# Linear attention: the order of the score-value and state matmuls in a chunk

## The chip, the cores and the metric

The kernel runs on one core of a Trainium2 chip. The metric is the device time of one execution in microseconds (us); lower is better. Engines are named as the profile names them: PE (TensorE), PEld (its weight loads), DVE (VectorE), ACT (ScalarE), POOL (GpSimd), SP (the engine whose queue starts most transfers).

## What is computed

One decoder layer on 512 tokens of width 1024: a mixer with two branches (gated linear attention, GLA, and a sparse softmax attention) and then a mixture of 32 experts. The change touches the GLA branch only. Its reference, cut to one chunk and one head:

```python
b = cumsum(la)                                   # log decay inside the chunk
o_inter = (q * exp(b)) @ state                   # the state carried into the chunk
scores = einsum('td,sd,tsd->ts', q, k, decay)    # causal, decayed
o = o_inter + scores @ v
state = exp(b_last) * state + (k * exp(b_last - b)).T @ v
```

There are 4 heads with 64 key and 128 value columns. The kernel uses chunks of 128 tokens, so there are TT = 4 chunks, numbered 0 to 3.

## The kernel before

All data is fp32. A matmul on plain fp32 operands is executed as two passes, so the profile counts two PE instructions for each of them; weight products are instead written out by hand as three matmuls on rounded operands (lines 480 to 482), one pass each.

The semaphores and the order of work are written by hand, one instruction list for each engine. Softmax attention and GLA are interleaved in one loop over units u = 0 to 16 (line 668). In unit u PE does, in this order: the attention scores of unit u (`attn_scores`, line 588, 64 contraction rows for each of two heads), the transposes of unit u-1 (`attn_turn`, line 598), `gla_out(ch)` if u is 9, 11, 13 or 15 (chunk 0, 1, 2 or 3), one eighth or so of a weight product as filling (lines 480 to 482), `gla_turn(ch-1)` in even units from 10 (line 660), the attention output of unit u-1 (`attn_out`, line 611), and `gla_scores(ch)` in units 8, 10, 12 and 14 (lines 620 and 627). DVE, ACT and POOL walk the same units in their own lists.

`gla_out(ch)` (line 632) is where the change is. It takes the PSUM banks G and O, head pair member hh = 0 writing to G and hh = 1 to O, each in two column halves r = 0 and 1. For each of the four heads it issues, from chunk 1 on, a state matmul (line 642: 64 contraction rows, SBUF rows 0 to 63 for hh = 0 and rows 64 to 127 for hh = 1) and right behind it a score-value matmul (line 643: 128 contraction rows) that adds to the same columns. Then, except in the last chunk, it forms the chunk's contribution to the state (line 652) in one of the banks T0 and T1, which take turns. The profile writes an instruction's rows and columns of the array before the shape: 64\*128, 128\*128 or 128\*64.

What reads the results: ACT squares the four heads of o (line 1441, `gla_squares`), DVE makes the norm (lines 1727, 1951, 1957, `gla_norm`) and frees G and O, DVE updates the state (line 1942), and POOL starts the exponents of the next chunk (lines 1193 and 1195, `gla_exponents`) when both banks are full, because these exponents overwrite the factors that the state matmuls read; line 1206 on POOL follows. ACT copies the first head's transposed probabilities out of a T bank (line 1469, freed at line 1471), DVE the second's (line 1992). ACT copies the attention output out of bank O (line 1481), and `gla_scores` takes G and O after that. DVE scales the probabilities at line 2002.

Weights come through a ring: the SP queue starts the load of an item when PE has signalled that an earlier item is used up (`ring_out`, waited for before line 994 and the lines after it), and the first expert weights (line 1032) wait for the end of the output projection in the same way.

Of the kernel before, what the change touches and what calls it, by code (L numbers as in the profile page):

```python
# [24 lines left out]
P = 128  # L25
# [56 lines left out]
def layer(nc, x, c, positions, w_ada, b_ada, g_pre_mix, g_post_mix, g_pre_ffn, g_post_ffn, w_in,  # L82
# [17 lines left out]
    with ExitStack() as ctx:  # L100
# [20 lines left out]
        expo = qi_mem[:, 0:1792].rearrange("p (r n) -> p r n", r=2)  # L121
# [11 lines left out]
        gv = gvs[:, 0:2048].rearrange("p (t n) -> p t n", t=TT)  # L133
# [23 lines left out]
        scT = gla_mem[:, 1024:1536].rearrange("p (h n) -> p h n", h=4)  # L157
        kN = gla_mem[:, 1536:1792]
        state = gla_mem[:, 1792:2048].rearrange("p (r n) -> p r n", r=2)
# [141 lines left out]
        ps, bank = {}, {}  # L301
# [87 lines left out]
        def _(pe):  # L389
            def take(name, turn):  # L390

                n = bank[name].turn(turn)
                if n:
                    pe.wait_ge(bank[name].free, n)
                return ps[name]
# [3 lines left out]
            def take_next(kind, turn):  # L399
                name = f"{kind}{flip[kind] % 2}"  # L400
                flip[kind] += 1
                where[turn] = name
                return take(name, turn), bank[name].full
# [11 lines left out]
            for k in range(KD):  # L415
                t, full = take_next("T", ("x", k))
                for tt in range(TT):
                    if k == 0:
                        pe.wait_ge(xn_ready, tt + 1)
                    last = nc.tensor.transpose(t[:, tt * P:(tt + 1) * P], x_in[:, tt, k * P:(k + 1) * P], ident[:, :])  # L420
# [108 lines left out]
            for tt in range(TT):  # L529
                a, full = take_next("A", ("small", tt))  # L530
                for k in range(KD):
                    last = nc.tensor.matmul(a[:, 0:NS], hT[:, k, tt * P:(tt + 1) * P], w_small[:, k, :], start=(k == 0), stop=(k == KD - 1))
# [11 lines left out]
            for tt in range(TT):  # L544
                last = nc.tensor.transpose(t[:, tt * P:(tt + 1) * P], kin[:, tt, :, :].rearrange("p a n -> p (a n)"), ident[:, :])
            last.then_inc(full, 1)
            t, full = take_next("T", "ga")
            for tt in range(TT):
                last = nc.tensor.transpose(t[0:RANK, tt * P:(tt + 1) * P], ikw[:, tt, 0:RANK], ident[:, :])
# [14 lines left out]
            for n in range(3 * PAIRS):  # L564
                index_scores(1 + n // PAIRS, n % PAIRS)
                if n in (1, 3):

                    r = n // 2
# [63 lines left out]
            def gla_out(ch):  # L632
                pe.wait_ge(sc_ready, 2 * ch + 2)
                pe.wait_ge(gv_ready, TT)
                o = [take(n, ("o", ch)) for n in ("G", "O")]
                if ch:
                    pe.wait_ge(state_ready, 2 * ch)
                for r in range(2):
                    for hh in range(2):
                        h, lo = 2 * r + hh, 64 * hh  # L640
                        if ch:
                            nc.tensor.matmul(o[hh][:, r * P:(r + 1) * P], expo[lo:lo + 64, r, 640:768], state[lo:lo + 64, r, :], start=True, stop=False)
                        last = nc.tensor.matmul(o[hh][:, r * P:(r + 1) * P], scT[:, h, :], gv[:, ch, h * P:(h + 1) * P], start=(ch == 0), stop=True)
                        if r == 1:
                            last.then_inc(bank["GO"[hh]].full, 1)
                if ch < TT - 1:
                    pe.wait_ge(kN_ready, ch + 1)
                    t, full = take_next("T", ("state", ch))
                    for r in range(2):
                        for hh in range(2):  # L650
                            h = 2 * r + hh
                            last = nc.tensor.matmul(t[64 * hh:64 * hh + 64, r * P:(r + 1) * P], kN[:, r * P + 64 * hh:r * P + 64 * hh + 64],
                                                    gv[:, ch, h * P:(h + 1) * P], start=True, stop=True)
                    last.then_inc(full, 1)
# [13 lines left out]
            for u in range(NU + 1):  # L668
                ch, odd = (u - GLA_AT) // 2, (u - GLA_AT) % 2
                if u < NU:  # L670
                    attn_scores(u)
                if u:
                    attn_turn(u - 1)
                if odd and 0 <= ch < TT:
                    gla_out(ch)
                if fill:
                    fill.pop(0)()
                if not odd and 0 < ch <= TT:
                    gla_turn(ch - 1)
                if u:  # L680
                    attn_out(u - 1)
                if not odd and 0 <= ch < TT:
                    gla_scores(ch)
# [1730 lines left out]
```

## Time and profile before

| what | value |
|---|---|
| three timed runs | 791.08, 793.13, 793.21 us; median 793.13 us |
| the profiled execution: its span | 789.2 us, 9728 instructions |
| PE | 703.0 us busy (89%) |
| PE weight loads | 447.0 us (57%) |
| DVE / ACT / POOL | 411.7 (52%) / 287.7 (36%) / 120.9 us (15%) |
| the GLA chunks' `gla_out` on PE | between 248.3 and 327.6 us of the span |

No other time of the profiled execution is given than its span, which covers the first to the last instruction. The median lies 3.9 us above it. The profile's PE clock is the clock that was granted to TensorE, as a share of 2.4 GHz. A busy PE is not a PE at its peak: a matmul's record lasts from its start to its modelled end and records overlap, so what a matmul costs is read from the distance between starts.

### The profile page before, as it was taken

To read this page: it belongs to the slowest core of one execution; us is meant where nothing else is said; L and a number is where in the kernel's file an instruction comes from. 1 tells how busy PE (TensorE), PEld (TensorE's weight loads), DVE (VectorE), ACT (ScalarE), POOL (GpSimd) and SP (SyncE) were. 2 spreads that over 40 slices of the span, in tenths; PEclk is the share of its full clock that TensorE was granted. 3 is DMA by queue.
4 is the path that set the end of the run, shared out by engine and by line. 5 is a ranking of instruction groups with operands and counts; after the bars stand their busy time and mean duration, and the time that the engine had idled before them with its cause. 6 is when DMAs were issued, how large, how long until landed. Compare 5 with 4: busy or idle time off the path is not lost.

```text
span 789.2 us, 9728 instructions
## 1 busy us (share of the span) xinstructions
PE 703.0 (89%) x3451; PEld 447.0 (57%) x3451; DVE 411.7 (52%) x876; ACT 287.7 (36%) x514; POOL 120.9 (15%) x148
## 2 busy tenths in 40 slices
PE   1799989998998999999999899989979978878784
PEld 0347747666776777777787678873423323323221
DVE  2386858998897665654422636572533211112118
ACT  5233255254447768642022315344112211112223
POOL 3064852210002022000000000101121221111100
PEclk9999989999999889999999999999989998989997
DMA  9989730411302030023334472599999999999982
GB/s 337 396 311 364 283 142 1 116 44 64 107 9 99 1 107 1 5 104 107 107 123 161 142 267 79 229 374 391 418 422 418 420 419 419 421 420 413 409 327 108
DMA packets 50300, 179.27 MB, mean 227 GB/s; under 512 B 9624, under 2 KB 13826, under 8 KB 36428
## 3 DMA queue, kind: packets, MB, share of 16 engines
q1 hardware_dynamic: 44308, 166.26, 54.1%
q0 software_dynamic: 4784, 8.19, 2.9%
q10 hardware_dynamic: 1160, 4.20, 1.4%
q8 instruction: 28, 0.46, 0.2%
q14 instruction: 20, 0.16, 0.1%
HBM read 174.13 MB, written 12.59 MB: 237 GB/s over the span
## 4 chain that ended last, share of the span: by engine, by line
PE 48%; SPq 13%; DVE 13%; DMA 8%; ACT 4%; issue 3%; POOL 0%; DVEq 0%; ACTq 0%; POOLq 0%; PEldq 0%
PE psA L480 10%; PE psA L482 10%; PE psA L481 10%; SPq L1032 5%; SPq L1090 4%; SPq L1040 4%; PE psS L884 3%; PE psA L913 3%; DMA arena<-in_w_e_up_dram 2%; PE psG L884 2%; DVE mk_mem L1846 2%; DMA y_dram<-sig_mem,tables 2%; DVE m L1845 2%; PE psO L611 1%; PE psT L598 1%
## 5 line engine op out<-in xcount | busy, mean ns | idle before, releaser
L480 PE MATMUL psA<-arena_r 128*128 128x512 f32 x320 | 130.8, 409 | 3.5 <-DVE arena_r L1794 2.9
L481 PE MATMUL psA<-arena_r 128*128 128x512 f32 x320 | 127.0, 397 | 0.0
L482 PE MATMUL psA<-arena_r 128*128 128x512 f32 x320 | 126.8, 396 | 0.0
L1794 DVE TENSOR_TENSOR arena_r<-arena,arena_r 128x1024 fp32r<-128x1024 f32 (+1 forms) x37 | 60.4, 1654 | 38.4 <-ACT arena_r L1313 37.4
L480 PEld LDWEIGHTS psA<-arena_r 128*128 128x128 f32 x320 | 61.5, 192 | 24.4 <-issue 12.3
L482 PEld LDWEIGHTS psA<-arena_r 128*128 128x128 f32 x320 | 61.5, 192 | 13.5
L481 PEld LDWEIGHTS psA<-arena_r 128*128 128x128 f32 x320 | 61.5, 192 | 12.2 <-issue 0.2
L884 PE MATMUL psG<-arena,kv 128*64 128x512 f32 x208 | 61.2, 642 | 7.6 <-issue 7.6
L884 PE MATMUL psS<-arena,kv 128*64 128x512 f32 x224 | 58.5, 611 | 9.8 <-issue 7.9
L1313 ACT CAST arena_r<-arena 128x1024 fp32r<-128x1024 f32 (+1 forms) x31 | 49.9, 1630 | 20.6 <-DMA arena<-in_w_in_dram 10.2
L913 PE MATMUL psA<-qs_mem,sig_mem 128*64 128x512 f32 x80 | 39.5, 637 | 4.4 <-ACT sig_mem L1637 4.4
L2291 DVE TENSOR_TENSOR sig_mem<-sig_mem,psS 128x256 f32<-128x256 f32 x8 | 4.9, 613 | 72.7 <-ACT sig_mem L1632 72.7
L1239 POOL DMA_INDIRECT y_dram<-sig_mem,tables x16 | 15.9, 994 | 174.6 <-issue 108.5
L480 PE MATMUL psA<-arena_r,qs_mem_r 128*128 128x512 f32 x96 | 38.1, 397 | 4.2 <-DVEq L2037 3.3
L2291 DVE TENSOR_TENSOR sig_mem<-sig_mem,psG 128x256 f32<-128x256 f32 x8 | 4.9, 612 | 70.7 <-ACT sig_mem L1632 70.7
L884 PEld LDWEIGHTS psS<-arena,kv 128*64 128x64 f32 x224 | 20.1, 140 | 37.4 <-issue 36.9
L884 PEld LDWEIGHTS psG<-arena,kv 128*64 128x64 f32 x208 | 19.6, 147 | 33.5 <-issue 32.8
L472 PE MATMUL psA<-arena,kv 128*128 128x512 f32 x64 | 29.2, 619 | 2.3 <-DMA arena<-in_w_in_dram 2.3
L481 PE MATMUL psA<-arena_r,qs_mem_r 128*128 128x512 f32 x80 | 31.1, 389 | 0.0
L1646 ACT COPY sig_mem<-psA 128x512 f32<-128x512 f32 x16 | 9.4, 586 | 55.7 <-PE psA L913 32.2
L1411 ACT ACTIVATE sig_mem<-psA 128x512 f32<-128x512 f32 x16 | 9.6, 598 | 50.8 <-PE psA L482 50.8
L1845 DVE MAX8 m<-mk_mem 128x8 f32<-128x256 f32 (+2 forms) x48 | 26.9, 560 | 2.2
(443 smaller groups left out, 1304.2 us busy)
## 6 DMA issues: line engine op xcount, KB each, us to landing
arena<-in_w_e_gate_dram SPq DMA_DIRECT2D x24, 1024.0 KB, 17.0
arena<-in_w_e_up_dram SPq DMA_DIRECT2D x24, 1024.0 KB, 19.4
arena<-in_w_in_dram SPq DMA_DIRECT2D x11, 2048.0 KB, 8.8
arena<-in_w_e_down_dram SPq DMA_DIRECT2D x12, 1024.0 KB, 18.6
qs_mem<-in_w_e_down_dram SPq DMA_DIRECT2D x10, 1024.0 KB, 23.0
arena<-in_w_ada_dram SPq DMA_DIRECT2D x4, 2048.0 KB, 16.8
qT<-in_w_ada_dram SPq DMA_DIRECT2D x6, 1024.0 KB, 5.4
gvs<-in_w_ada_dram SPq DMA_DIRECT2D x5, 1024.0 KB, 6.3
```

Of the source, the lines that this page charges most:

```text
L472: last = nc.tensor.matmul(a[:, :], hT[:, k, tt * P:(tt + 1) * P], w[:, k, :], start=(k == 0), stop=(k == KD - 1))
L480: nc.tensor.matmul(acc, lhs[0], rhs[0], start=start, stop=False)
L481: nc.tensor.matmul(acc, lhs[0], rhs[1], start=False, stop=False)
L482: return nc.tensor.matmul(acc, lhs[1], rhs[0], start=False, stop=stop)
L884: last = nc.tensor.matmul(ps[g][64 * q:64 * q + 64, :].rearrange("p (g f) -> p g f", g=2), h2g[:, b, k, 64 * q:64 * q + 64], gu, start=(k ...
L913: last = nc.tensor.matmul(ps[name][64 * q:64 * q + 64, :], actT[:, b, kf, 64 * q:64 * q + 64], down_sets[z][q][:, D * kf + 512 * n:D * kf ...
L1032: sp.dma_start(dst, src[bass.ds(e, 1), :, :].rearrange("a p n -> p (a n)")).then_inc(we_in[z], 16)
L1040: sp.dma_start(down_sets[z][q], wed_v[bass.ds(e, 1), :, :].rearrange("a p n -> p (a n)")).then_inc(wd_in[z], 16)
L1090: sp.dma_start(gu_sets[z][q][:, 2048 * n:2048 * (n + 1)][:, part], src[2 * j + q][:, part]).then_inc(we_last[j - (NPAIR - 2)] if half else ...
L1313: nc.scalar.copy(hi[:, part], src[:, part]).then_inc(hi_ready, 4 if q is None else 1)
L1794: V.tensor_tensor(lo[:, part], src[:, part], hi[:, part], ALU.subtract).then_inc(lo_ready, 4 if q is None else 1)
L1845: step(V.max(m8[:, :], work))
```

## The change

The four score-value matmuls of a chunk come first, the four state matmuls behind them, after the wait for the state (line 637), which moves between the two groups. Each bank is now one accumulation group: the first matmul into a bank has the start flag, all later ones in it, also those on the other column half, have not. The signal that a bank is full moves to the last state matmul of that bank; in chunk 0, which has no state matmuls, it stays on the last score-value matmul. Number, shapes and operands of the matmuls are the same.

```diff
                 o = [take(n, ("o", ch)) for n in ("G", "O")]
+                for r in range(2):
+                    for hh in range(2):
+                        h = 2 * r + hh
+                        last = nc.tensor.matmul(o[hh][:, r * P:(r + 1) * P], scT[:, h, :], gv[:, ch, h * P:(h + 1) * P], start=(r == 0), stop=(ch == 0 and r == 1))
+                        if r == 1 and ch == 0:
+                            last.then_inc(bank["GO"[hh]].full, 1)
                 if ch:
                     pe.wait_ge(state_ready, 2 * ch)
-                for r in range(2):
-                    for hh in range(2):
-                        h, lo = 2 * r + hh, 64 * hh
-                        if ch:
-                            nc.tensor.matmul(o[hh][:, r * P:(r + 1) * P], expo[lo:lo + 64, r, 640:768], state[lo:lo + 64, r, :], start=True, stop=False)
-                        last = nc.tensor.matmul(o[hh][:, r * P:(r + 1) * P], scT[:, h, :], gv[:, ch, h * P:(h + 1) * P], start=(ch == 0), stop=True)
-                        if r == 1:
-                            last.then_inc(bank["GO"[hh]].full, 1)
+                    for r in range(2):
+                        for hh in range(2):
+                            lo = 64 * hh
+                            last = nc.tensor.matmul(o[hh][:, r * P:(r + 1) * P], expo[lo:lo + 64, r, 640:768], state[lo:lo + 64, r, :], start=False, stop=(r == 1))
+                            if r == 1:
+                                last.then_inc(bank["GO"[hh]].full, 1)
```

## Rows read from the trace of the kernel before

**Rows 1.** The page, part 4: the chain that ended last, shares by engine.
```profile
PE 48%; SPq 13%; DVE 13%; DMA 8%; ACT 4%; issue 3%; POOL 0%; DVEq 0%; ACTq 0%; POOLq 0%; PEldq 0%
```
**Rows 2.** Windows: stretch, its length, busy us (instructions) by engine, PEclk, DMA share, GB/s.
```profile
160.00:345.00 185.00, 175.88 (x1013) 132.13 (x1009) 140.67 (x346) 108.85 (x219) 18.70 (x21) 0.95 0.16 58
537.00:760.00 223.00, 192.04 (x908) 73.66 (x904) 55.24 (x135) 43.96 (x109) 29.29 (x29) 0.95 1.00 408
```
**Rows 3.** Timeline of PE, chunks 2 and 3: start us, us, engine, line, operation.
```profile
298.29 1.14 PE L588 MATMUL psS<-kv,qT 64*128 64x512 f32 x4
299.36 1.09 PE L598 MATMUL psT<-ident,qs_mem 128*128 128x128 f32 x8
300.38 0.48 PE L642 MATMUL psG<-gla_mem,qs_mem 64*128 64x128 f32 x2
...
303.71 0.66 PE L652 MATMUL psT<-gvs,gla_mem 128*64 128x128 f32 x8
...
324.46 0.48 PE L642 MATMUL psG<-gla_mem,qs_mem 64*128 64x128 f32 x2
...
327.62 0.47 PE L480 MATMUL psA<-arena_r 128*128 128x512 f32 x1
```
**Rows 4.** Timeline of PE: matmuls of one kind behind each other.
```profile
199.38 0.49 PE L588 MATMUL psS<-kv,qT 64*128 64x128 f32 x4
199.80 0.44 PE L598 MATMUL psT<-ident,qs_mem 128*128 128x128 f32 x2
...
248.63 0.39 PE L643 MATMUL psO<-gvs,gla_mem 128*128 128x128 f32 x2
248.85 0.39 PE L643 MATMUL psG<-gvs,gla_mem 128*128 128x128 f32 x2
```
**Rows 5.** Timeline of PE in chunk 1, then a window (PE busy, PEclk, DMA).
```profile
271.86 1.06 PE L598 MATMUL psT<-ident,qs_mem 128*128 128x128 f32 x4
272.85 0.80 PE L642 MATMUL psG<-gla_mem,qs_mem 64*128 64x128 f32 x2
...
278.64 1.12 PE L652 MATMUL psT<-gvs,gla_mem 128*64 128x128 f32 x8
...
281.00:282.00 1.00, 1.00 (x4) 0.76 0.00 0
```
**Rows 6.** Timelines of ACT and PE: the copy that frees a T bank.
```profile
250.43 0.46 ACT L1469 COPY sig_mem<-psT 128x384 f32<-128x384 f32 x1
251.07 1.12 PE L652 MATMUL psT<-gvs,gla_mem 128*64 128x128 f32 x8 [1.62 <-ACTq L1471]
...
302.16 0.56 ACT L1469 COPY sig_mem<-psT 128x512 f32<-128x512 f32 x1
```
**Rows 7.** Timelines of DVE and POOL in chunk 0, where both work at once.
```profile
251.43 1.01 DVE L2002 TENSOR_SCALAR qs_mem<-qs_mem,sm 128x384 f32<-128x384 f32 x1
...
250.98 1.25 POOL L1193 TENSOR_TENSOR qs_mem<-gla_mem 128x512 f32<-128x512 f32 x1
```
**Rows 8.** Timelines of ACT and PE behind chunk 2; in brackets idle time and its end.
```profile
311.11 0.27 ACT L1481 COPY qT<-psO 128x128 f32<-128x128 f32 x1 [0.36 <-PE psO L611]
...
320.14 0.27 ACT L1481 COPY qT<-psO 128x128 f32<-128x128 f32 x1 [0.24 <-PE psO L611]
...
320.59 0.26 PE L627 MATMUL psG<-qs_mem 64*128 64x32 f32 x1
```
**Rows 9.** Timelines of ACT, DVE and PE behind chunk 3.
```profile
327.97 0.28 ACT L1441 ACTIVATE gla_mem<-psO 128x128 f32<-128x128 f32 x1 [0.53 <-PE psO L643]
...
331.95 0.34 DVE L1957 SCALAR_TENSOR_TENSOR gla_mem<-psO,st,gvs 128x128 f32<-128x128 f32 x1
...
335.81 0.69 DVE L1992 COPY sig_mem<-psT 128x512 f32<-128x512 f32 x1 [0.92 <-PE psT L598]
...
333.65 1.09 PE L611 MATMUL psO<-sig_mem,kv 128*64 128x128 f32 x16 [0.30 <-PE psA L482]
```
**Rows 10.** Waits of the SP queue: us in total, times, longest us.
```profile
SPq L1032 <- PEq L774: 43.0, 1, 43.0
```

## The prediction, made before the changed kernel ran

> **What bounds the kernel now.** I read the chain of work that ended last first: PE holds 48% of it, the SP queue 13% and DVE 13% [rows 1]. The table of windows then says where. In the attention and GLA stretch (160 to 345 us) PE is busy 175.88 of 185 us while no other engine and no DMA is near its limit; in the expert stretch (537 to 760 us) the DMA engines are full, at 408 GB/s [rows 2]. So a microsecond of PE time saved in GLA is worth one if two things hold: nothing else in the unit loop becomes late, and the DMA-bound stretch starts earlier too. The second holds: the first expert load that the queue waits for (it waited 43.0 us) is released by PE at the end of the output projection [rows 10], and the loads of the ring before it are released by PE in the same way. What starts the full stretch moves with PE, so I carry the saving to the end in full. The rest is the unit loop.
>
> **What the change removes.** Number and shape of the matmuls stay. What goes is the change of tiling (64 rows, 128 rows, 64 rows...) between neighbours. The timeline of PE gives its price at full clock. From the first state matmul of chunk 2 to the state update there are eight groups of two passes in 303.71 - 300.38 = 3.33 us, 0.416 us a group [rows 3]. The same score-value pairs without state matmuls between them, in chunk 0, start 0.22 us apart (248.63, 248.85), 0.11 a pass [rows 4]. Eight transposes of the same tiling take 299.36 to 300.38, 1.02 us until the next tiling starts, so leaving the tiling costs 1.02 - 0.88 = 0.14 [rows 3].
>
> The 64-row group of eight passes has no row of its own; the nearest are the attention scores, which also alternate between the two row halves and two banks. Four passes of 128 columns take 0.42 us until the next tiling (199.38 to 199.80) [rows 4], four of 512 columns 1.07 (298.29 to 299.36) [rows 3]. That is 0.054 us a pass of 128 columns and 0.20 fixed, so eight passes take 0.63 us. The bounds are 0.42 (the two halves stream at once) and 8 x 0.11 + 0.20 = 1.08 (no overlap of loads); I take 0.63, since both rows lie on that line. The rows of 512 columns show no doubling: 4 x 512 columns at 2.4 GHz are 0.85 of the 1.07 us. The Trainium skill (TensorEngine Tiling (Array Packing), Theoretical Speedup) says on the contrary that a contraction of at most 64 rows gives up to twice the rate, as two tiles work at once. By that page the group would take some 0.2 us less at full clock and twice that at half clock. The row decides, as it is fp32 work of the very same form.
>
> **Chunk 2, at full clock.** The score-value group no longer needs the 0.14 after the transposes: it starts at 300.38 - 0.14 = 300.24, takes 0.88 + 0.14, and the state group ends its turn at 301.26 + 0.63 = 301.89, where before it was 303.71. That is 1.8 us on PE, but not all of it can be used. The state update takes a T bank that ACT frees, and in chunk 0, where the group is already dense, this is what PE waits for: 1.62 us, and it starts 0.18 after ACT's copy ends (250.89 to 251.07) [rows 6]. In chunk 2 that copy ends at 302.16 + 0.56 = 302.72 [rows 6], and it hangs on exps and attention scores, not on `gla_out`. So the state update starts at 302.90: 0.8 us are left on PE, and it idles 1.0.
>
> Something is late next. POOL starts the next exponents when G and O are full: about 302.1 instead of 303.9. That now falls on DVE's two scalings of the probabilities (line 2002, 302.7 to 303.7). In chunk 0 this overlap exists: a scaling of 0.42 took 1.01 us beside a POOL instruction that itself took 1.25 [rows 7]. One or two such hits delay DVE's mean square, ACT's square root, and with it all of ACT's list, which has only 0.36 + 0.24 = 0.6 us of idle up to the copy of the attention output at 320.14; the scores of chunk 3 on PE start 0.18 after that copy ends [rows 8]. If the norm runs d us later than before, chunk 2 saves at most 0.6 - d: with d between 0 and 1.0 that is +0.6 to -0.4. With d = 0.5 (one hit, as in chunk 0) I take 0.1 us. The Trainium skill (SBUF — State Buffer, Who interferes with whom) says that GpSimd and a VectorE instruction in a two-port mode exclude each other for the whole instruction, whoever starts first. By that page both scalings would wait, d would be 1.0, and the sum 0.5 us worse; in chunk 0 the first of the two ran undisturbed, so I keep one hit.
>
> **Chunk 3.** 324.46 to 327.62 before, with no state update behind it [rows 3]. After: 324.32 + 0.88 + 0.14 + 0.63 = 325.97, when the weight product starts. 1.65 us. POOL has no exponents behind the last chunk. ACT's squares lose the 0.53 us that they wait for bank O [rows 9], so the norm ends about 0.6 us earlier, at 331.7, and frees bank O for the attention output, which PE reaches at 333.65 - 1.65 = 332.0 [rows 9]: just in time. In unit 16 DVE's copy has 0.92 us of idle ahead of it [rows 9]; PE comes 1.65 earlier, DVE's list only 0.6, so about 0.1 is lost. 1.5 us remain.
>
> **Chunk 1, at half clock.** Here the granted clock is down: four transposes from 271.86 take 0.213 us each (starts up to 272.50), a little over twice the 0.11 before; the mixed groups take (278.64 - 272.85) / 8 = 0.72 us, and the clock is back only between 281 and 282 us (mean 0.76) [rows 5]. By the same working: the transposes end their turn at 272.50 + 0.21 = 272.71; score-value 8 x 0.213 = 1.70 and 0.14 to leave, 274.56; state 8 x 0.107 + 0.25, rounded 1.1, so 275.7. Before it was 278.64: 3.0 us. ACT's copy that frees the T bank ends at 274.4, so PE does not wait for it, and POOL starts at 276, when DVE has ended its scalings at 275.6. The clock came back some 2 us after the weight product had begun (279.7 to 281.5), and I let it do so again relative to that start; then the product costs the same. If it comes back only when it did, the product runs 3 us more at half clock and 1.4 of the 3.0 are lost; if the denser group brings it back before the product, up to 1.2 us are added. I take 3.0. What hangs on it later (DVE's attention mask in unit 12 has 0.7 us of idle, ACT's list starts from PE's attention output) moves along.
>
> **Edits at nothing.** Chunk 0 has the same matmuls in the same order; only start flags differ. The wait for the state now stands in front of the second group; DVE writes the state a whole chunk earlier, so it is never the last to come, and it would cost what is queued on PE behind it if it were. No DMA and no SP or POOL instruction is moved in its list.
>
> **Sum.** 3.0 + 0.1 + 1.5 = 4.6 us. On the profiled execution 789.2 - 4.6 = 784.6 us; the median is 3.9 us above that span, so 793.13 - 4.6 = 788.5 us.
>
> **Rivals.**
> (a) The clock is not down in chunk 1 in the runs that are timed, since where it falls may differ from run to run. At full clock PE would be done with the group at 273.7, then wait for the T bank until 274.62, against 275.5 before: 0.9 instead of 3.0. 793.13 - (0.9 + 0.1 + 1.5) = 790.6 us. For it: in chunks 2 and 3 the clock stayed up. Against: the only trace has it down.
> (b) The clock comes back sooner, or falls more often before the change than this trace shows: +1.2 for chunk 1 and up to 1.3 more for each other chunk that was at half clock: 786 us.
> (c) The saving does not arrive: ACT's list, with 0.24 to 0.36 us of idle in units 13 and 14 [rows 8], sets the pace of the units and PE only idles more (chunk 2 is such a case already), or the full DMA stretch starts no earlier. 793 us. Against: the chain goes through PE in units 11 and 15, and the SP queue waits for PE [rows 10].
> (d) Slower: the clock. In chunk 0 it fell while PE idled 1.6 us ahead of the state update [rows 6]. The change makes such a pause of 1.0 us in chunk 2 and removes PE time everywhere. If the clock falls in chunk 2 and again in chunk 3, each time for as long as in chunk 1 (10 us, in which the work of 6 us at full clock is done, so 4 us lost), the sum is -4.6 + 2 x 4 = +3.4: 796.5 us. It decides from the second extra fall on. Against: the pause is shorter than the 1.6 us, and dense work follows it.
>
> **Chances.** Forecast (3.0 to 6 us saved) 0.47, (a) 0.27, (b) 0.10, (c) 0.11, (d) 0.05. The measurement of this kernel can tell about 0.3%, 2.4 us, from no change. (a) lies on that limit: I give half of it to faster. Faster 0.47 + 0.10 + 0.12 = 0.69, same 0.15 + 0.11 = 0.26, slower 0.05. The range must reach over (a) with chunk 2 at its worst end (0.9 - 0.4 + 1.5 = 2.0 saved, 791.1) and the spread of the three runs (about 1 us each side), and down to (b): 785.8 to 792.0. (d) and most of (c) are left out.
>
> **What would show it.** In the new trace: line 643 in chunks 1 to 3 at 0.11 us a pass at full clock (wrong if 0.2); line 642 eight passes in about 0.63 us, with G and O records interleaved; in chunk 2 a wait of PE's line 652 for line 1471 of about 1 us; POOL's line 1193 in chunk 2 starting before DVE's line 2002, and a line 2002 or 1727 of more than 0.7 us; line 480 after chunk 3 1.6 us earlier relative to the transposes. The first expert loads must start earlier by the whole saving. The prediction is wrong if the group is dense and the end does not move, if line 642 costs as much as before (the tiling is not what costs), or if the windows show a half clock in chunks 2 and 3.

## The result

| | kernel before | changed kernel | ratio, 95% interval |
|---|---|---|---|
| median of 10 and 10 executions | 791.27 us (789.75 to 796.73) | 786.24 us (784.71 to 789.48) | 0.9942 [0.9922, 0.9963] |
| the same two kernels on another chip, 23 and 12 executions | 789.49 us (785.43 to 796.11) | 787.14 us (785.08 to 790.02) | 0.9963 [0.9937, 0.9988] |
| the profiled execution: span | 789.2 us | 784.8 us | |
| distance of time and span in it | not known | 786.7 - 784.8 = 1.9 us | |

The change makes the kernel faster, by 0.58% in the first comparison and by 0.37% in the second. The span is 4.4 us shorter. The page's chain and the windows of the changed kernel, beside [rows 1] and [rows 2] (the expert stretch begins 4 us earlier, so the second window is moved by 4):

```profile
PE 51%; DVE 14%; DMA 8%; ACT 6%; issue 5%; SPq 5%; DVEq 0%; POOL 0%; ACTq 0%; POOLq 0%; PEldq 0%
```
```profile
160.00:345.00 185.00, 174.03 (x1047) 132.71 (x1046) 144.31 (x350) 112.67 (x223) 19.35 (x21) 0.98 0.17 58
533.00:756.00 223.00, 192.05 (x904) 74.33 (x902) 55.23 (x135) 43.97 (x109) 29.23 (x29) 0.95 1.00 408
```

PE still holds the chain, and ACT has more of it (6% for 4%). In the stretch bound by DMA the rate is the same, 408 GB/s. The 1.9 us in the last row of the table, taken for the kernel before too, put its profiled execution at some 791.1 us (an estimate), 2 us below the median of three from which the forecast starts. PE's list in chunk 2 (columns as in [rows 3]):

```profile
294.66 1.09 PE L598 MATMUL psT<-ident,qs_mem 128*128 128x128 f32 x8
295.59 0.39 PE L639 MATMUL psG<-gvs,gla_mem 128*128 128x128 f32 x2
295.81 0.39 PE L639 MATMUL psO<-gvs,gla_mem 128*128 128x128 f32 x2
...
296.57 0.37 PE L647 MATMUL psG<-gla_mem,qs_mem 64*128 64x128 f32 x1
296.58 0.37 PE L647 MATMUL psO<-gla_mem,qs_mem 64*128 64x128 f32 x1
...
298.21 0.66 PE L656 MATMUL psT<-gvs,gla_mem 128*64 128x128 f32 x8 [0.93 <-ACTq L1475]
```

and in chunk 3, down to the next attention output:

```profile
318.03 1.09 PE L598 MATMUL psT<-ident,qs_mem 128*128 128x128 f32 x8
318.96 0.39 PE L639 MATMUL psG<-gvs,gla_mem 128*128 128x128 f32 x2
...
319.95 0.37 PE L647 MATMUL psG<-gla_mem,qs_mem 64*128 64x128 f32 x1
...
320.59 0.50 PE L480 MATMUL psA<-arena_r 128*128 128x512 f32 x1
...
326.63 1.09 PE L611 MATMUL psO<-sig_mem,kv 128*64 128x128 f32 x16 [0.30 <-DVEq L1965]
```

Inside the diff, line 643 has become 639 and 642 has become 647; everything behind the diff is four lines lower, so 652 is 656 and 1471 is 1475. The score-value matmuls run at 0.11 us a pass (0.22 from 295.59 to 295.81). The 64-row passes of the two banks start together and four such pairs with the way out take 320.59 - 319.95 = 0.64 us. Chunk 3 takes 320.59 - 318.96 = 1.63 us, where it took 327.62 - 324.46 = 3.16.

How far a piece of work moved from one trace to the other does not show the saving, because the clock of PE falls at other places in them. So the table below takes distances between two starts on PE, at full clock unless it is said, for both traces of each kernel (the second trace of the kernel before comes from the run r0_before, that of the changed kernel from r1_after).

| from, to (starts on PE) | before | before again | changed | changed again |
|---|---|---|---|---|
| chunk 1: attention scores of unit 11, of unit 12 | 16.88 (half clock) | 12.51 | 11.57 | 11.59 |
| chunk 2: transposes of unit 13, scores of unit 15 | 23.01 | 23.02 | 22.30 | 22.30 |
| chunk 3: transposes of unit 15, next attention output | 10.21 | 10.21 | 8.60 | 8.60 |

At equal clock the changed kernel saves 0.93, 0.71 and 1.61 us, 3.25 us together. The whole way from the scores of unit 11 to the last of these starts agrees: 58.82 us in r0_before, 55.53 and 55.59 in the two traces of the changed kernel. The 16.88 of the first trace holds 4.4 us that the clock cost, not the order of the matmuls.

### The profile page after: what moved, and what is told of

Its sections match the earlier page's. It is cut to its first block, busy times and chain, and to the rows that moved or that the text cites. A ratio compares the mean times of both kernels' runs of the same rounds, so it can differ in the third digit from the quotient of the medians.

```text
span 784.8 us, 9728 instructions
## 1 busy us (share of the span) xinstructions
PE 694.6 (88%) x3451; PEld 442.2 (56%) x3451; DVE 411.7 (52%) x876; ACT 287.3 (37%) x514; POOL 121.7 (16%) x148
## 4 chain that ended last, share of the span: by engine, by line
PE 51%; DVE 14%; DMA 8%; ACT 6%; issue 5%; SPq 5%; DVEq 0%; POOL 0%; ACTq 0%; POOLq 0%; PEldq 0%
PE psA L480 10%; PE psA L481 9%; PE psA L482 9%; PE psS L888 6%; PE psA L917 5%; SPq L1094 4%; PE psG L888 4%; DMA arena<-in_w_e_up_dram 3%; DVE mk_mem L1850 2%; DMA y_dram<-sig_mem,tables 2%; DVE m L1849 2%; DMA xn_dram<-sig_mem 1%; DMA arena<-in_w_out_dram 1%; DMA kv<-xn_dram,tables 1%; ACT arena_r L1317 1%
## 5 line engine op out<-in xcount | busy, mean ns | idle before, releaser
L888 PE MATMUL psS<-arena,kv 128*64 128x512 f32 x224 | 63.1, 648 | 12.2 <-issue 9.8
L888 PE MATMUL psG<-arena,kv 128*64 128x512 f32 x208 | 58.2, 612 | 4.8 <-issue 4.8
L480 PE MATMUL psA<-arena_r,qs_mem_r 128*128 128x512 f32 x96 | 39.3, 409 | 4.5 <-DVEq L2041 3.7
L481 PE MATMUL psA<-arena_r,qs_mem_r 128*128 128x512 f32 x80 | 32.1, 401 | 0.0
L1636 ACT ACTIVATE sig_mem<-psS 128x256 f32<-128x256 f32 x8 | 3.1, 383 | 67.9 <-PE psS L888 67.8
```

The costliest lines, as they stand in the source:

```text
L480: nc.tensor.matmul(acc, lhs[0], rhs[0], start=start, stop=False)
L481: nc.tensor.matmul(acc, lhs[0], rhs[1], start=False, stop=False)
L888: last = nc.tensor.matmul(ps[g][64 * q:64 * q + 64, :].rearrange("p (g f) -> p g f", g=2), h2g[:, b, k, 64 * q:64 * q + 64], gu, start=(k ...
```

## Where the clock falls

The windows of the first trace of the kernel before, of its second trace (r0_before) and of the changed kernel, around chunk 0, chunk 1 and the router; columns as in [rows 2], the granted clock is the third number from the end:

```profile
250.00:260.00 10.00, 8.93 (x48) 6.85 (x48) 6.23 (x16) 7.88 (x18) 3.18 (x5) 0.83 0.01 2
270.00:280.00 10.00, 10.00 (x48) 6.96 (x47) 3.80 (x12) 3.70 (x14) 1.14 (x2) 0.56 0.01 2
436.00:448.00 12.00, 8.65 (x39) 6.84 (x38) 7.56 (x9) 7.13 (x2) 0.00 (x0) 1.00 0.54 170
```
```profile
250.00:260.00 10.00, 9.29 (x35) 7.12 (x36) 5.86 (x16) 6.71 (x17) 2.34 (x4) 0.66 0.01 2
270.00:280.00 10.00, 10.00 (x78) 7.67 (x77) 4.65 (x16) 6.35 (x18) 3.21 (x5) 1.00 0.01 2
```
```profile
250.00:260.00 10.00, 8.38 (x46) 6.47 (x44) 6.70 (x18) 8.11 (x19) 3.10 (x4) 0.83 0.01 2
270.00:280.00 10.00, 9.12 (x76) 7.43 (x75) 5.62 (x19) 6.92 (x17) 4.31 (x5) 1.00 0.01 2
436.00:448.00 12.00, 11.17 (x38) 9.00 (x39) 7.55 (x11) 1.14 (x1) 0.00 (x0) 0.73 0.00 0
```

The same unchanged kernel has 0.56 of the clock in chunk 1 in one trace and all of it in the other. The changed kernel's trace is the mirror of the first: full clock in chunk 1, 0.73 at the router, where the kernel before had 1.00. So its lead over the first trace is 343.33 - 336.31 = 7.0 us behind the unit loop, and only 454.97 - 450.92 = 4.05 behind the router (the same router matmul in both); 4.4 are left at the end.

This also goes with much of the spread of the times. Over the 46 executions of the kernel before whose clock is on record (on two chips; for the ten of the first comparison it is not), time and mean granted clock go together (correlation -0.81): 785.43 us at 0.972, 796.11 us at 0.955. One straight line for each kernel with a common slope, over these 46, the 22 of the changed kernel and 12 of a third one (e5 below), gives 3.85 us per 0.01 of clock (standard error 0.41), and at a clock of 0.965 the times 789.82 us before and 786.59 us changed. The difference is -3.24 us with a standard error of 0.36. The ratios make it 791.27 x 0.0058 = 4.6 and 789.49 x 0.0037 = 2.9 us, on either side of it. The trace's 3.25 us and the fit's 3.24 us come from different numbers, the one from starts on PE inside single traces, the other from the times of whole executions. That they are so near each other is partly luck: the same fit over the one chip on which both kernels were timed side by side with their clock on record gives -2.2 us with a standard error of 0.5.

## The experiments

Five of the experiments have a single execution (e1, e2, e3, e4 and e6). Its time tells little: e3's 789.12 us came with a mean clock of 0.959, e2's 786.82 us with 0.968. They are read by distances inside their traces, at full clock.

**r0_before** is the kernel before once more. What was expected:

> The kernel before once more, unchanged, to see where the granted clock falls in other executions. In its first trace the clock was down from 271.2 to 281.5 us (chunk 1) and at 250.8 to 254.2 (chunk 0); in the trace of the changed kernel only the second of these was there, and another stood at 436 to 448 us. Theory A (where it falls is chance, the change has no part in it): the fall in chunk 1 is missing or elsewhere here, the stretch from the scores of unit 11 (line 588) to the transposes of unit 12 (line 598) takes about 13.2 us instead of 17.9, and the kernel's own saving is 0.9 + 0.7 + 1.6 = 3.2 us. Theory B (the mixed order itself lowers the clock in chunk 1): the fall is there again at about 271 us. Ratio to before 1.000 within 0.003 in both.

It took 789.98 us, the kernel before beside it 790.01 (ratio 0.9992 [0.9964, 1.002]). Its mixed groups in chunk 1:

```profile
273.24 0.48 PE L642 MATMUL psG<-gla_mem,qs_mem 64*128 64x128 f32 x2
...
276.57 0.66 PE L652 MATMUL psT<-gvs,gla_mem 128*64 128x128 f32 x8
```

3.33 us, exactly what chunk 2 took before [rows 3]; in the first trace it was 278.64 - 272.85 = 5.79 [rows 5]. From the scores of unit 11 to the transposes of unit 12 it took 13.57 us, near the 13.2 of Theory A and far from 17.9. So the kernel before need not lose the clock in chunk 1. That the order of the matmuls has no part in where it falls is not shown. Over all ten traces the clock fell in chunk 1 in two of the four with the mixed order (the first one and e1, 0.83 between 270 and 280 us) and in one of the six with the sorted order (e5); in chunk 0 it fell in all of them but e5.

**r1_after** is the changed kernel once more, in five rounds beside e5.

> The changed kernel once more, unchanged, timed in five rounds beside the kernel before on one chip. Theory A (the clock falls by chance, the change saves PE time alone): 3.2 to 4.5 us less, ratio 0.994 to 0.996, at an equal mean clock in both. Theory B (the change also keeps the clock up): the mean clock is at least 0.003 higher than that of the kernel before and the saving is over 4.5 us.

787.14 us against 789.49, as in the table above: 2.35 us less and a ratio of 0.9963, just outside what Theory A gave. The mean clock was 0.9657 against 0.9637, so 0.002 higher, less than the 0.003 of Theory B. Whether the change keeps the clock up by so little stays open.

**e1_full_rows** keeps the old mixed order, but lets the state matmuls contract all 128 rows. This adds the other head's state, which the reference does not, so its output differs; number and length of the passes are the same. So the tiling no longer changes inside the group, while order, flags and the number of matmuls are the old ones.

```diff
-nc.tensor.matmul(o[hh][...], expo[lo:lo + 64, r, 640:768], state[lo:lo + 64, r, :], start=True, stop=False)
+nc.tensor.matmul(o[hh][...], expo[:, r, 640:768], state[:, r, :], start=True, stop=False)
```

> The order of the kernel before (state and score-value matmuls in turn), but every state matmul contracts over all 128 rows, so no tiling changes inside the group; it adds the other head's state as well, which is not what the reference computes. Theory 1 (the change of tiling is the cost): sixteen passes at 0.11 us, 1.76 us and 0.14 to leave, 1.9 us for a chunk at full clock instead of 3.33; eight pair groups 0.22 us apart. Rival (the cost is in switching the accumulation between start and no start on the same columns, or in alternating operands): the groups stay 0.42 us apart, 3.3 us.

One execution took 785.53 us. Its PE in chunk 2:

```profile
296.99 0.39 PE L642 MATMUL psG<-gla_mem,qs_mem 128*128 128x128 f32 x2
297.21 0.39 PE L643 MATMUL psG<-gvs,gla_mem 128*128 128x128 f32 x2
...
299.61 0.66 PE L652 MATMUL psT<-gvs,gla_mem 128*64 128x128 f32 x8 [0.68 <-ACTq L1471]
```

A group of two passes costs 0.22 us instead of 0.416 in the old order. The change of tiling is the whole price of that order; neither the alternation of state and score-value matmuls nor the start flags have a part in it. In chunk 1 the clock was down in this trace, and there the groups start 0.43 us apart.

**e2_state_first** has the two groups of the change the other way round: state first, score-value behind it.

> As the changed kernel, but the four state matmuls come first and the four score-value matmuls behind them. Theory 1 (only the number of tiling changes counts): from the end of the transposes to the state update's earliest start the same 1.7 us as in the changed kernel (0.14 + 0.63 + 0.88 + 0.14); in chunk 3, with the weight product of the same tiling behind it, 0.14 less than the changed kernel. Rival (score-value first matters, because it needs no state): at least 0.3 us longer in some chunk, as PE would wait for the state.

786.82 us in one execution. In chunk 2:

```profile
297.40 0.37 PE L641 MATMUL psG<-gla_mem,qs_mem 64*128 64x128 f32 x1
...
299.93 0.66 PE L654 MATMUL psT<-gvs,gla_mem 128*64 128x128 f32 x8 [0.73 <-ACTq L1473]
...
299.68 1.00 DVE L2004 TENSOR_SCALAR qs_mem<-qs_mem,sm 128x512 f32<-128x512 f32 x1
...
299.35 1.05 POOL L1195 TENSOR_TENSOR qs_mem<-gla_mem 128x512 f32<-128x512 f32 x1 [18.74 <-PE psO L645]
```

In chunk 3 it takes 1.56 us from the first state matmul to the product (320.93 to 322.49), and 2.59 from the transposes (319.90); the changed kernel takes 2.56 (318.03 to 320.59). The 0.14 us that Theory 1 expected to gain in chunk 3 did not come, and PE never waited for the state. So on PE it is the number of tiling changes that counts, not which group stands first. In chunk 2 the state update starts 3.55 us behind the transposes in both kernels, but the scores of unit 15 come after 22.46 us instead of 22.30. The last two rows show a longer collision on DVE than the changed kernel has (see e4).

**e3_halves_apart** issues the state matmuls as both of bank G and then both of bank O, so that neighbours in PE's list no longer sit on different row halves.

```diff
-                    for r in range(2):
-                        for hh in range(2):
+                    for hh in range(2):
+                        for r in range(2):
```

> As the changed kernel, but the state matmuls of rows 0 to 63 (bank G) come first, both column halves, then those of rows 64 to 127 (bank O). Theory 1 (the two row halves overlap only when they alternate): the eight passes of line 647 take 8 x 0.11 + 0.20 = 1.08 us until the next group where nothing is waited for (chunk 3), instead of 0.63, and the saving in chunk 3 falls from 1.6 to about 1.2 us. Rival (order among the halves does not matter, since the passes overlap over four matmuls anyway): 0.63 us again.

789.12 us in one execution. Chunk 3:

```profile
322.19 0.37 PE L647 MATMUL psG<-gla_mem,qs_mem 64*128 64x128 f32 x1
322.21 0.37 PE L647 MATMUL psO<-gla_mem,qs_mem 64*128 64x128 f32 x1
322.41 0.27 PE L647 MATMUL psG<-gla_mem,qs_mem 64*128 64x128 f32 x1
322.42 0.27 PE L647 MATMUL psO<-gla_mem,qs_mem 64*128 64x128 f32 x1
...
322.84 0.50 PE L480 MATMUL psA<-arena_r 128*128 128x512 f32 x1
```

My theory was wrong and the rival right: 322.84 - 322.19 = 0.65 us, and the passes still start in pairs. The O passes stand fifth to eighth in the list and start with the first to fourth. The two row halves take their work side by side, even when the list does not alternate. All four pairs do so, in chunks 1 and 2 as well.

**e4_pool_later** lets POOL's next exponents wait until DVE has ended its scalings, so that the two no longer overlap in chunks 0 to 2.

```diff
                 if ch:
+                    pool.wait_ge(p_ready, 2 * (GLA_AT + 2 * ch - 1) + 2)
                     filled(pool, ("o", ch - 1), "G")
```

> The changed kernel, but POOL starts a chunk's exponents only when DVE has scaled the unit's probabilities (line 2006). Theory 1 (POOL and DVE at once cost DVE time): in chunk 2 the first scaling takes 0.49 us instead of 0.84, the mean square (line 1731) ends about 0.4 us earlier, and the scores of chunk 3 start 0.4 us earlier relative to the transposes of unit 13. Rival (POOL's later start collides with the mean square instead): the mean square takes over 0.6 us and nothing is won or up to 0.5 us is lost.

787.77 us in one execution. First DVE, POOL and ACT of the changed kernel in chunk 2, then of e4:

```profile
297.96 0.84 DVE L2006 TENSOR_SCALAR qs_mem<-qs_mem,sm 128x512 f32<-128x512 f32 x1
298.91 0.49 DVE L2006 TENSOR_SCALAR qs_mem<-qs_mem,sm 128x512 f32<-128x512 f32 x1
...
300.06 0.27 DVE L1731 TENSOR_SCALAR st<-st 128x4 f32<-128x4 f32 x1
...
297.47 1.05 POOL L1197 TENSOR_TENSOR qs_mem<-gla_mem 128x512 f32<-128x512 f32 x1 [18.61 <-PE psO L647]
...
299.03 1.28 POOL L1197 TENSOR_TENSOR qs_mem<-gla_mem 128x512 f32<-128x512 f32 x1
...
297.46 0.56 ACT L1473 COPY sig_mem<-psT 128x512 f32<-128x512 f32 x1
298.14 0.28 ACT L1445 ACTIVATE gla_mem<-psG 128x128 f32<-128x128 f32 x1
```
```profile
300.26 0.49 DVE L2007 TENSOR_SCALAR qs_mem<-qs_mem,sm 128x512 f32<-128x512 f32 x1
300.86 0.49 DVE L2007 TENSOR_SCALAR qs_mem<-qs_mem,sm 128x512 f32<-128x512 f32 x1
...
302.04 0.46 DVE L1732 TENSOR_SCALAR st<-st 128x4 f32<-128x4 f32 x1 [0.18 <-ACT gla_mem L1446]
...
301.42 1.05 POOL L1198 TENSOR_TENSOR qs_mem<-gla_mem 128x512 f32<-128x512 f32 x1 [18.89 <-DVE qs_mem L2007]
```

Both scalings take 0.49 us when POOL is held back; in the changed kernel the first takes 0.84. The collision costs 0.35 us on DVE. But now the mean square (line 1732) meets POOL and takes 0.46 us instead of 0.27, as the rival said in part, so it ends 5.54 us behind the transposes of unit 13 (at 296.96) instead of 5.67: 0.13 us earlier, where Theory 1 expected 0.4. Of this, 0.09 arrives: from the transposes of unit 13 to the scores of unit 15 e4 takes 22.21 us, the changed kernel 22.30. e2 shows the other direction: there the first scaling took 1.00 us, the mean square ended 5.83 us behind the transposes, and the same stretch took 22.46 us, so all of the 0.16 us arrived.

**e5_update_in_product** issues the state update inside the weight product behind it (after two of its k steps in chunk 0, after one in chunks 1 and 2), so that PE has work while it waits for the T bank.

```diff
                 for k in range(KD):
+                    if hook is not None and k == hook[0]:
+                        hook[1]()
...
-                    fill.pop(0)()
+                    fill.pop(0)((1 if ch else 2, lambda ch=ch: gla_update(ch)))
```

> The changed kernel with the state update (line 656) issued inside the weight product that follows it, after two of its eight blocks in chunk 0 and after one in chunks 1 and 2, so that PE does not stand idle until ACT frees the T bank. Theory 1 (the three waits of 1.6, 0.9 and 0.9 us are what is left of the cost, as far as ACT's and DVE's lists have room): chunk 0 gives up to 1.1 us (ACT's idle in unit 9), chunk 1 0.4 to 0.7, chunk 2 nothing since ACT has no idle behind it; the clock fall in chunk 0 goes with the idle PE, which is worth up to 1.5 more; 1.5 to 3.3 us less than the changed kernel. Rival (ACT's and DVE's lists set the pace in units 9 to 14, PE only idles elsewhere): within 0.5 us of the changed kernel.

787.21 us in five rounds (ratio to the kernel before 0.9961 [0.9936, 0.9986]); the changed kernel on the same chip took 787.14. At equal clock, in the fit above, e5 is 0.13 us faster than the changed kernel, with a standard error of 0.50: no difference. Theory 1 expected 1.5 to 3.3 us; the rival's "within 0.5 us" holds for the time. The waits moved (the first row is a window, its clock the third number from the end):

```profile
250.00:260.00 10.00, 9.49 (x60) 6.95 (x61) 7.23 (x21) 8.42 (x19) 3.11 (x4) 1.00 0.01 2
...
252.63 0.66 PE L660 MATMUL psT<-gvs,gla_mem 128*64 128x128 f32 x8 [0.23 <-ACTq L1482]
...
269.24 0.26 PE L629 MATMUL psG<-qs_mem 64*128 64x32 f32 x1 [1.65 <-ACTq L1494]
...
274.95 0.63 PE L641 MATMUL psG<-gvs,gla_mem 128*128 128x128 f32 x2
275.38 0.64 PE L641 MATMUL psO<-gvs,gla_mem 128*128 128x128 f32 x2
...
317.60 0.26 PE L629 MATMUL psG<-qs_mem 64*128 64x32 f32 x1 [0.90 <-ACTq L1494]
```

In chunk 0 the wait for the T bank shrinks from 1.62 [rows 6] to 0.23 us and in chunk 2 it is gone, but PE then waits 1.65 and 0.90 us for ACT's copies ahead of the next chunk's scores. From unit 13's transposes to unit 15's scores e5 takes 22.31 us, the changed kernel 22.30. So in chunk 2, at full clock, ACT's list sets the pace, and PE's pause only stands in another place. For chunks 0 and 1 this is not shown, because the clock differs. In chunk 0 it stayed up in e5, and the scores of chunk 1 (line 629) started 21.33 us behind the transposes of unit 9, in the changed kernel 22.28. The 0.95 us were lost again at once, when the clock fell behind the pause of 1.65 us.

**e6_last_chunk_only** has the new order in chunk 3 and the old one in chunks 0 to 2.

> The new order in chunk 3 alone, the old one in chunks 1 and 2. Theory 1 (chunk 3 is worth 1.6 us by itself): from the first transposes of unit 15 to the attention output of unit 14 (line 611) 8.6 us as in the changed kernel, against 10.2 before; the loss of a little of it to bank O stays. Rival (chunk 3 only gains because the chunks before shifted the lists of ACT and DVE): less than 1.2 us.

787.8 us in one execution. In chunk 3:

```profile
318.72 1.09 PE L598 MATMUL psT<-ident,qs_mem 128*128 128x128 f32 x8
...
327.34 1.09 PE L611 MATMUL psO<-sig_mem,kv 128*64 128x128 f32 x16 [0.30 <-DVEq L1977]
```

8.62 us for the 10.21 before (333.65 - 323.44), and 23.01 in chunk 2, as in the old order. Chunk 3 gives its 1.6 us by itself: half of the whole saving.

## Why the prediction was right, and where its steps were not

788.5 us was forecast and 786.24 measured; 4.6 us were to be saved, against 5.0 between the medians and 3.2 at equal clock. The starting median of three executions, 793.13, was itself high: ten gave 791.27. Why the medians are 5.0 us apart and not 3.2 is not shown; the clock of those ten is not on record. Step by step:

- **What bounds.** Right. The queue's wait for PE at the end of the output projection is still there, so the loads start with PE:

```profile
SPq L1036 <- PEq L778: 42.0, 1, 42.0
```

  The `w_out` load moved from 428.73 to 421.71 us (7.0, as PE's work behind the unit loop), the first expert load from 513.84 to 508.62 (5.2), the next from 538.84 to 533.61 (5.2). "Earlier by the whole saving" holds within what the clock adds and takes in between.
- **Chunk 3, 1.5 us.** Right; 1.61 measured, and alone in e6. The 0.1 us that I took off for DVE's list in unit 16 is not lost: from the attention output to the output projection's first matmul it is 9.68 us before (333.65 to 343.33) and 9.68 after (326.63 to 336.31).
- **The 64-row group, 0.63 us.** Right (0.64), but one sentence behind it was wrong: that the rows of 512 columns show no doubling. I counted one column a cycle. The first projection, float32 on all 128 rows, shows what a pass of 512 columns costs:

```profile
57.59 5.31 PE L472 MATMUL psA<-arena,kv 128*128 128x512 f32 x12
```

  Its last record lasts 0.59, so eleven distances take 4.72 us, 0.43 each: two cycles a column. Four 64-row passes of 512 columns at that rate would be 1.72 us, and they took 1.07 [rows 3]. The doubling is there at both sizes; 0.054 us is just half of the 0.11 of a full pass. The Trainium skill (TensorEngine Tiling (Array Packing), Theoretical Speedup) names up to twice the rate for up to 64 rows, and these traces agree with it, beside some 0.2 us for the change of tiling. The 0.14 us for leaving the 128-row tiling was a little too high: with no change behind them the eight transposes take 0.93 us (294.66 to 295.59) and not 0.88, so leaving cost 1.02 - 0.93 = 0.09.
- **Chunk 2, 0.1 us.** The mechanism was right, the size was off: 0.71. PE's part came as worked out: the attention output stands 9.81 us behind the transposes (304.47 - 294.66), before 10.61 (309.97 - 299.36), which is the forecast 0.8, and the wait for the T bank is 0.93 us where 1.0 was forecast. The failed term is d, taken as 0.5 with bounds 0 and 1.0. POOL did start before DVE's first scaling (297.47 and 297.96) and did slow it (0.84). But I left out what the same early banks do to ACT. In ACT's timeline of the kernel before, in chunk 2, the squares waited for both banks:

```profile
302.99 0.28 ACT L1441 ACTIVATE gla_mem<-psG 128x128 f32<-128x128 f32 x1 [0.26 <-PE psG L643]
...
303.88 0.28 ACT L1441 ACTIVATE gla_mem<-psO 128x128 f32<-128x128 f32 x1 [0.53 <-PE psO L643]
```

  Now they follow the copy with no wait (298.14 behind 297.46 + 0.56). The squares gain 0.63 us, the collision takes some of it back, and the norm's mean square ends 5.67 us behind the transposes, where it ended at 6.01. d was -0.34. The lower bound of 0 had no reason behind it. ACT's list was then nearly no limit: it was 0.09 us short of PE's 0.80, and this is the collision, as e4 shows, where all 0.80 arrive (23.01 - 22.21).
- **Chunk 1, 3.0 us.** This held for the one trace I had and not as a rule. At full clock it is 0.93, rival (a)'s 0.9, with the wait at the T bank (0.88 us). The half-clock price itself was never seen whole after the change. One part fits: in e5 the clock was down in chunk 1, and the score-value matmuls stood 0.43 us apart (274.95 to 275.38) where the mixed ones took 0.72 [rows 5]. The state group at half clock stays unmeasured. The weight that I gave (a), 0.27, was too low: a term that hangs on where the clock falls in one trace should have been entered at its full-clock value.
- **Rivals (c) and (d).** ACT's list does set the pace in chunk 2, as (c) said, but from a point that lies behind the change's saving and not before it; only further PE time (e5) is worth nothing there. The clock did not fall because of PE's pauses of 0.88 and 0.93 us in chunks 1 and 2 in either trace of the changed kernel. It fell in chunk 0 in all four traces of the two kernels, in three of them behind pauses of 1.10 and 1.62 us close to each other, in r1_after already behind the first of 1.73 and 1.18 us. In e5 the second pause is 0.23 us and the clock stayed up there, but it fell at 270 us, behind the pause of 1.65. That points to long pauses; the dip in chunk 1 of the first trace, behind a pause of only 0.36 us (268.71, for ACT), speaks against it as the only cause, and no run settles it.
- **POOL and DVE.** One hit, as the prediction kept. The Trainium skill (SBUF — State Buffer, Who interferes with whom) says that between GpSimd and a VectorE instruction in a two-port mode whoever issues first holds the shared ports for its whole instruction, while the other is blocked. That both scalings would then wait, as I worked it out, does not follow. The first scaling (297.96) started behind POOL's instruction (297.47) and was late; the second (298.91) started ahead of POOL's next long one (299.03), and there POOL took longer, 1.28 us instead of 1.05. The size, too, roughly agrees with this: POOL's instruction had 0.56 us left when the first scaling started, which took 0.35 us more than its 0.49; in e2 0.72 us were left and the scaling took 0.51 more.

So 3.0 + 0.1 + 1.5 was in truth 0.93 + 0.71 + 1.61 at equal clock. The first term was too high by 2.1, the second too low by 0.6, so the sum was 1.35 us too large. It came near the 5.0 us between the medians only because 1.8 us of those come from something other than these matmuls, and that is luck. With full clock in chunk 1 the prediction's own sum is rival (a)'s, 790.6 us.

## What to carry to other kernels

Look in PE's timeline for neighbours with different tilings (64*128 beside 128*128): each change cost 0.09 to 0.20 us at full clock here, at the upper end nearly as much as two passes of 128 columns, and sorting the matmuls by tiling inside an accumulation group takes it away, whichever group is first. When a stage finishes earlier, ask of every reader of its banks whether it was waiting: a gain there can outweigh a collision that one has found. Before one prices work at a lowered clock, look at a second execution, and compare two kernels at equal mean clock: 0.01 of it was worth 3.85 us here, more than the whole change.

## What was not expected of the hardware

Work on one row half of PE can overtake work on the other: four passes on the second half, issued behind four on the first, start together with them (322.19 and 322.21, e3). The cost of a change of tiling does not double at half clock: a mixed group costs 0.416 - 0.22 = 0.20 us more than an unmixed one at full clock and 0.72 - 0.43 = 0.29 at half clock (the 0.43 from e1 and e5), where twice as much would be 0.40. And the granted clock's dip of one and the same kernel lay in chunk 1 in one execution (0.56) and not in the next (1.00), with nothing else changed.
